# A 512-token transformer chain on one core: what stands at its stage boundaries

## The reference

```
# first block (8 heads per branch)
proj = rmsnorm(x) @ w_in       # A q,k,v | B q,f,i,g | C c_q,c_kv,k_rope | 3 gates
y_a = chunked_relpos_attention(a_q, a_k, a_v, rel_bias)
y_b = hgrn2_recurrence(b_q, b_f, b_i, b_g, ...)
y_c = mla_attention(c_q, c_kv, k_rope, ...)   # q = rmsnorm(c_q) @ w_uq, rotated
x = x + sum(sigmoid(gate_n) * (y_n @ w_branch[n])) @ w_out
x = x + relu(h2 @ w_ff1)**2 @ w_ff2
x = rmsnorm(x)
# second block, for each of two layers
x = x + mixer(rms_norm(x))     # stick-breaking, then differential attention
h = rms_norm(x)
x = x + (silu(h @ w_gate) * (h @ w_up)) @ w_down
```

## Time and profile before

| | |
|---|---|
| median of 3 runs | 2430.44 us (2429.25 to 2431.67) |
| the profiled execution's own time | 2428.63 us |
| its span | 2426.7 us |
| TensorE busy | 2289.7 us, 94% |
| VectorE, ScalarE, GpSimd busy | 1271.0, 932.8, 253.4 us |
| mean granted TensorE clock | 0.984 |

### The profile page before, as it was taken

One profiled execution on the slowest core, in us unless ns is written; L12 is line 12 of the kernel. 1 busy time (PEld: TensorE's weight loads), 2 busy tenths in 40 slices (PEclk: granted clock), 3 DMA queues, 4 the chain that ended last, 5 costly groups with the idle time before them and its releaser, 6 DMA issues.

```text
span 2426.7 us, 26942 instructions
## 1 busy us (share of the span) xinstructions
PE 2289.7 (94%) x10372; PEld 1779.0 (73%) x10372; DVE 1271.0 (52%) x2010; ACT 932.8 (38%) x1558; POOL 253.4 (10%) x422
## 2 busy tenths in 40 slices
PE   7999999898999999999998899999999888999999
PEld 6767777665888888877564688888776656888887
DVE  4574564355554544463444555555545766555554
ACT  4353332444443323242535433333344544433332
POOL 0000121220210000020313200000133201000000
PEclk9999999999999999999999999999999999999999
DMA  4212101211322222322110132323222101233223
GB/s 160 70 44 74 48 27 40 75 42 44 122 96 96 96 99 91 105 78 87 36 61 18 53 101 96 99 96 96 87 70 70 52 27 44 96 96 104 96 96 104
DMA packets 52110, 187.47 MB, mean 77 GB/s; under 512 B 5904, under 2 KB 6032, under 8 KB 51856
## 3 DMA queue, kind: packets, MB, share of 16 engines
q1 hardware_dynamic: 51984, 185.76, 23.5%
HBM read 183.64 MB, written 2.10 MB: 77 GB/s over the span
## 4 chain that ended last, share of the span: by engine, by line
PE 82%; ACT 6%; DVE 5%; POOL 3%; issue 3%; DMA 0%; POOLq 0%; DVEq 0%; SPq 0%; ACTq 0%
PE ps L774 20%; PE ps L777 20%; PE ps L775 20%; PE ps L795 3%; PE ps L798 3%; PE ps L796 3%; PE ps L865 2%; PE ps L897 2%; PE ps L759 2%; PE ps L943 1%; PE ps L974 1%; ACT W L1386 1%; ACT W L1384 1%; PE ps L1075 1%; ACT wh L1140 1%
## 5 line engine op out<-in xcount | busy, mean ns | idle before, releaser
L774 PE MATMUL ps<-hh,wl 128*128 128x512 f32 x1408 | 570.8, 405 | 21.9 <-DVE wl L1438 11.6
L1438 DVE TENSOR_TENSOR wl<-raw,wh 128x1024 fp32r<-128x1024 f32 (+1 forms) x336 | 421.4, 1254 | 301.8 <-ACT wh L1140 301.2
L777 PE MATMUL ps<-hl,wh 128*128 128x512 f32 x1408 | 552.7, 393 | 0.0
L775 PE MATMUL ps<-hh,wh 128*128 128x512 f32 x1408 | 552.2, 392 | 0.0
L1140 ACT CAST wh<-raw 128x1024 fp32r<-128x1024 f32 (+1 forms) x336 | 350.6, 1044 | 408.7 <-PE ps L777 315.5
L774 PE MATMUL ps<-R,wl 128*128 128x512 f32 x896 | 362.7, 405 | 4.3 <-issue 3.6
L777 PE MATMUL ps<-R,wh 128*128 128x512 f32 x896 | 352.4, 393 | 0.0
L775 PE MATMUL ps<-R,wh 128*128 128x512 f32 x896 | 351.8, 393 | 0.0
L774 PEld LDWEIGHTS ps<-hh,wl 128*128 128x128 f32 x1408 | 267.1, 190 | 83.6 <-issue 28.3
L777 PEld LDWEIGHTS ps<-hl,wh 128*128 128x128 f32 x1408 | 266.6, 189 | 58.0 <-DVE hl L1516 0.4
L775 PEld LDWEIGHTS ps<-hh,wh 128*128 128x128 f32 x1408 | 267.2, 190 | 54.9 <-issue 2.6
(11 more groups left out here) (225 smaller groups left out, 2376.7 us busy)
## 6 DMA issues: line engine op xcount, KB each, us to landing
raw<-in_weights SPq DMA_DIRECT2D x332, 512.0 KB, 3.3
x<-in_x_t SPq DMA_DIRECT2D x4, 512.0 KB, 6.4
F<-in_x_t SPq DMA_DIRECT2D x4, 512.0 KB, 5.3
out<-x SPq DMA_DIRECT2D x8, 256.0 KB, 2.0
raw<-in_weights SPq DMA_DIRECT2D x4, 416.0 KB, 3.2
x<-in_bias SPq DMA_DIRECT2D x1, 1024.0 KB, 6.0
C<-in_consts SPq DMA_DIRECT2D x1, 832.0 KB, 6.7
F<-in_weights SPq DMA_DIRECT2D x2, 384.0 KB, 3.6
```

Of the source, the lines that this page charges most:

```text
L774: pe.matmul(out, lo[:, k, cs], xh, start=k == 0, stop=False)
L775: pe.matmul(out, hi[:, k, cs], xh, start=False, stop=False)
L777: last = pe.matmul(out, hi[:, k, cs], xl, start=False, stop=k == u.nk - 1)
L1438: dve.tensor_tensor(lo, src, hi.bitcast(F32), ALU.subtract).then_inc(S[name], 1)
```

## The change

Seven edits to the plan, none of which adds or removes a dense matmul.

1. The last units of a stage take banks of their own where the next stage takes others: the last unit of A's projections and that of `uv[0]` take 0, 1, 6, 7; `bf` takes 4, 5, 6, 7; the q, k, v units `ud[0]` of differential attention go through six banks.
2. The recurrence's last four steps move from the end of uGA into uC, and the rest is spread at 44/48 instead of 48/48. uC takes banks 0, 1, 4, 5.
3. `c_norm` makes its eight squares first, then two logarithms and one exponential for all four token tiles. Before, it made two of each for every tile. Its squares go to W4 to W7, and VectorE's scaling waits for all of them.
4. In the latent branch each group's order is now `c_q`, `c_kv`, `c_qt`, `c_kt`, and `c_turn` begins one step later.
5. GpSimd rotates the queries two token tiles at a time: 12 operations per group on 128 columns, where 24 on 64 stood.
6. Group two's sixteen steps are attached to steps 4 to 19 of attention C0. Its heads go to F4 and F0 instead of F1 and F3, so that C0 can still read its own. The ratio is 66/48 instead of 75/48, since 19 ticks of side work have gone; attention C1 then ends with uGB.
7. The gated feed-forward's chunks have 2, 4, 4, 4, 4 and 4 tiles.

```diff
+C_HEADS = (("F1", "F3"), ("F4", "F0"))
...
     def mla(self):
+
+        def steps(g):
+            return [[(n, g, i)] for n in ("c_q", "c_kv", "c_qt", "c_kt") for i in range(4)]
+
+        yield []
         yield []
         for j in range(3):
             yield [("c_turn", j)]
         yield [("c_rope",)]
-        for g in range(2):
-            for tt in range(4):
-                yield [("c_q", g, tt)]
-            yield []
-            yield []
-            for h in range(4):
-                yield [("c_qt", g, h)]
-            for tt in range(4):
-                yield [("c_kv", g, tt)]
-            for h in range(4):
-                yield [("c_kt", g, h)]
-            yield from self.attn(ATTN[f"C{g}"])
+        yield from steps(0)
+        extra = [[]] * 4 + steps(1)
+        for i, tick in enumerate(self.attn(ATTN["C0"])):
+            yield tick + (extra[i] if i < len(extra) else [])
+        yield from self.attn(ATTN["C1"])
...
-                up, nj, f = [], 4 if c < 5 else 2, 8 + 6 * idx + c
+                up, k0, nj, f = [], max(4 * c - 2, 0), 4 if c else 2, 8 + 6 * idx + c
                 self.f_tile.append(tile)
                 for j in range(nj):
-                    gate = rows(("w_gate_2", idx), 0, 8, c * 512 + j * P, P, ("h", e), "fgate", wk=(4 * c + j) % 8)
-                    up += [gate, rows(("w_up_2", idx), 0, 8, c * 512 + j * P, P, ("h", e), "fup", gate=gate,
-                                      wk=(4 * c + j) % 8, f=f, j=j, tile=tile + j)]
-                ff.append((up, self.out(("w_down_2", idx), 4 * c, nj, ("f", f), norm=norm if c == 5 else None,
+                    c0, wk = (k0 + j) * P, (k0 + j) % 8
+                    gate = rows(("w_gate_2", idx), 0, 8, c0, P, ("h", e), "fgate", wk=wk)
+                    up += [gate, rows(("w_up_2", idx), 0, 8, c0, P, ("h", e), "fup", gate=gate, wk=wk, f=f, j=j,
+                                      tile=tile + j)]
+                ff.append((up, self.out(("w_down_2", idx), k0, nj, ("f", f), norm=norm if c == 5 else None,
                                         ship=idx == 1 and c == 5)))
                 tile += nj
...
-        self.run(self.dense(uA, roots(0, True) | {6: [("late",)], 9: [("late2",)]}))
+        self.run(self.dense(uA[:8], roots(0, True) | {6: [("late",)], 9: [("late2",)]}))
+        self.banks = (0, 1, 6, 7)
+        self.run(self.dense(uA[8:]))
         self.banks = (2, 3)
         self.run(interleave(self.dense(uB), self.attn(ATTN["A"]), 37 / 32))
         self.banks = (0, 1, 2, 3)
-        self.run(self.dense(uF))
+        self.run(self.dense(uF[:1]))
+        self.banks = (4, 5, 6, 7)
+        self.run(self.dense(uF[1:]))
         self.banks = (0, 1)
-        self.run(interleave(self.dense(uGA), self.hgrn(), 48 / 48))
-        self.banks = (0, 1, 2, 3)
-        self.run(self.dense(uC))
+        recurrence = list(self.hgrn())
+        self.run(interleave(self.dense(uGA), iter(recurrence[:-4]), 44 / 48))
+        self.banks = (0, 1, 4, 5)
+        self.run(self.dense(uC, {2 + 2 * i: t for i, t in enumerate(recurrence[-4:])}))
         self.add("c_norm")
         self.banks = (2, 3)
-        self.run(interleave(self.dense(uGB), self.mla(), 75 / 48))
+        self.run(interleave(self.dense(uGB), self.mla(), 66 / 48))
         self.banks = (0, 1, 2, 3)
         self.run(self.dense(uGC, {10 + 8 * i: [("again", i)] for i in range(4)}))
         self.run(self.dense(uO))
         self.run(self.dense(chain(ff1), roots(1)))
-        self.run(self.dense(uq[0] + uk[0] + uv[0], roots(2, True)))
+        self.run(self.dense(uq[0] + uk[0], roots(2, True)))
+        self.banks = (0, 1, 6, 7)
+        self.run(self.dense(uv[0]))
         self.banks = (2, 3)
         self.run(interleave(self.dense(uq[1] + uk[1]), self.sb(0), 18 / 32))
         self.banks = (0, 1, 2, 3)
...
         self.run(self.dense(uoS[1]))
         self.run(self.dense(chain(ff2a), roots(3)))
         self.add("zero", "F1", "F2")
+        self.banks = (0, 1, 2, 3, 4, 5)
         self.run(self.dense(ud[0], roots(4, True)))
+        self.banks = (0, 1, 2, 3)
         self.add("zero", "F5", "F6")
...
     def c_norm():
+        at.wait_ge("hg_s", 28)
         for tt in range(4):
-            o, w, s = B.F["F4"][:, tt * 416:(tt + 1) * 416], B.V(tt), B.stat(tt)
+            o, w, s = B.c_tokens()[:, tt, :], B.W[4 + tt], B.stat(tt)
             at.wait_ge(*plan.freed(plan.uC[0], tt)[0])
-            at.wait_ge("yb_l", 4)
             act.activation(w[:, 0:256], o[:, 0:256], ACT.Square, accum_out=s[:, 0:1]).then_inc(S["c_n"], 1)
             act.activation(w[:, 256:384], o[:, 256:384], ACT.Square, accum_out=s[:, 1:2]).then_inc(S["c_n"], 1)
-            for i, n in ((0, 256), (1, 128)):
-                at.wait_ge("c_n", 6 * tt + 1 + i)
-                act.activation(s[:, 2 + i:3 + i], s[:, i:i + 1], ACT.Ln, bias=eps, scale=1.0 / n).then_inc(S["c_n"], 1)
-                at.wait_ge("c_n", 6 * tt + 3 + 2 * i)
-                act.activation(s[:, 2 + i:3 + i], s[:, 2 + i:3 + i], ACT.Exp, scale=-0.5).then_inc(S["c_n"], 1)
+        s = B.st[:, 0:32].rearrange("p (t c) -> p t c", t=4)
+        at.wait_ge("c_n", 8)
+        act.activation(s[:, :, 2:3], s[:, :, 0:1], ACT.Ln, bias=eps, scale=1.0 / 256).then_inc(S["c_n"], 1)
+        act.activation(s[:, :, 3:4], s[:, :, 1:2], ACT.Ln, bias=eps, scale=1.0 / 128).then_inc(S["c_n"], 1)
+        at.wait_ge("c_n", 10)
+        act.activation(s[:, :, 2:4], s[:, :, 2:4], ACT.Exp, scale=-0.5).then_inc(S["c_n"], 1)
...
             if g:
-                at.wait_ge("at_o", ATTN["C0"].head(3))
+                at.wait_ge("c_t", 3)
+                at.wait_ge("c_rp", 6)
...
-            at.wait_ge("c_n", 6 * tt + 4)
+            at.wait_ge("c_n", 11)
             dve.tensor_scalar(o[:, 0:256], o[:, 0:256], s[:, 2:3], None, ALU.mult).then_inc(S["c_u"], 1)
-            at.wait_ge("c_n", 6 * tt + 6)
             dve.tensor_scalar(o[:, 256:384], o[:, 256:384], s[:, 3:4], None, ALU.mult).then_inc(S["c_u"], 1)
...
     def c_q(g, tt):
-        n = 24 * g + 6 * tt
-        o = B.c_heads("F0", tt)
-        w = B.F["F8"][:, 1280 + 256 * (tt % 2):1536 + 256 * (tt % 2)]
-        tmp = [w[:, 64 * i:64 * i + 64].rearrange("p (h r) -> p h r", h=4) for i in range(4)]
-        cos, sin = (B.misc_part(m).rearrange("p (t r) -> p t r", t=4)[:, tt, :].unsqueeze(1).to_broadcast([P, 4, 16])
+        if tt % 2 == 0:
+            return
+        o = B.F["F0"][:, (tt - 1) * 384:(tt + 1) * 384].rearrange("p (t h d) -> p t h d", t=2, h=4)
+        tmp = [B.F["F8"][:, 1280 + 128 * i:1408 + 128 * i].rearrange("p (t h r) -> p t h r", t=2, h=4) for i in range(4)]
+        cos, sin = (B.misc_part(m).rearrange("p (t r) -> p t r", t=4)[:, tt - 1:tt + 1, :].unsqueeze(2).to_broadcast([P, 2, 4, 16])
                     for m in ("cosA", "sinA"))
         at.wait_ge("c_qa", 4 * g + tt + 1)
-        rotate(o[:, :, 64:80], o[:, :, 80:96], o[:, :, 64:80], o[:, :, 80:96], cos, sin, tmp, "c_qp", n)
+        rotate(o[:, :, :, 64:80], o[:, :, :, 80:96], o[:, :, :, 64:80], o[:, :, :, 80:96], cos, sin, tmp, "c_qp",
+               12 * g + 6 * (tt // 2))
 
     def c_kv(g, tt):
```

15 lines of the change are left out of this document (9 added, 6 removed).

## The result

| | before | after |
|---|---|---|
| median of the runs | 2430.44 us (2429.25 to 2431.67) | 2438.39 us (2436.00 to 2444.00) |
| ratio to before, 95% interval | | 1.0036 (1.0025 to 1.0048) |
| profiled execution: span, clock | 2426.7 us, 0.984 | 2436.7 us, 0.981 |
| TensorE busy | 2289.7 us | 2298.9 us |

A forecast was written before the change was run, and what follows sets the result against it. TensorE was taken as the bound (busy 2289.7 of 2426.7 us), leaving its idle and half-clock time to win. Terms -7.6 - 0.8 - 2.5 - 1.1 + 1.5 - 4.5 + 2.0 = -13.0 gave a 2417.4 us median, range 2404 to 2427.

The forecast's parts named there:

- The short chunk first, six banks behind it: End of first gated feed-forward: late bank release behind the norm shrinks, -7.6 us (-9.2 to -5); kernel's end costs nothing.
- Banks of their own: Four other seams (behind A's projections, behind `uv[0]`, twice in `ud[0]`): 0.2 us each, -0.8, between 0 and -3.7.
- `bf`: Gate units: wait moves from bank to weights, half of the later `h_turn` wait goes; -2.5 us, between 0 and -3.5.
- The recurrence's end: In uC: its first matmul's wait goes, -1.1 us; moved `h_state` steps delay `h_out`, +1.5, between 0 and +5.
- `c_norm` and group one: Latent group one: shorter `c_turn` wait, rotation waits gone, new bank wait of 2.5; -4.5 us, between 0 and -7.
- Group two inside C0: Attention C0: sixteen steps wait 14.0 us for shared banks, 1.5 left in C1, against 13.5 lost before: +2.0 us.
- a low clock through C0: Many short waits make the clock fall across both attentions, 11.5 us lost: 2428.9, no change; chance 0.11.
- The slower rival: In C0, hand-overs cost like the dearest; at 2.4 us each the kernel takes 2441.8 us; chance 0.06.
- The signs of being wrong: Wrong if group two's waits add to half or double 14 us, or the norm's seam keeps 3 us.

## Why the prediction was wrong

Three steps of the sum failed: nothing was put for the last feed-forward's new order (it cost 5.0 us), the hand-overs in C0 were too small, and the clock was left out of the values. Of the loss 7 us more stand in stages that no edit explains. Taken by its own steps:

- *The short chunk first, six banks behind it* (-7.6): right for the first gated feed-forward, -8.2 in each profile. For the last one the step said "at the kernel's end the additions alone follow each tile, and they kept up before", and put the cost at nothing. **That conclusion failed.** The additions did keep up; what did not was the weight load, behind output transfers on SP's queue: +5.0, shown by the run that moves only those transfers. I had walked through VectorE's and ScalarE's queues at this place and not SP's.
- *Banks of their own* (-0.8) and *`bf`* (-2.5): the wait moved from the bank to the weights as forecast, 7.38. But the later wait shrank only to 0.71 and at another place, so 8.0 us of waits became 8.1. With the recurrence whole the same banks do give 1.7 (6.3 us of waits instead of 8.0), less than the 2.5 of the term; with the next edit beside them nothing is left.
- *The recurrence's end* (-1.1, +1.5): waits of 3.88, 2.83, 2.83 and 2.64 add up to 1.1 more than before, where 1.5 was forecast, and uC's 0.92 went as the -1.1 said. **The half-level clock behind them was put into the bound (+5) and not into the value**; measured, the part costs some 4.5 in all.
- *`c_norm` and group one* (-4.5): right in its waits, 2.15 at `c_turn` and 2.02 at `c_kv`, with those for the rotations gone. At 74 and 82 ticks over 48 the wait at `c_turn` is 3.0 to 3.6 in seven profiles, so the 2.15 holds for this spacing only.
- *Group two inside C0* (+2.0): **the walk through the hand-overs mis-sized the projections.** The transposes were put at 6.0 and waited 5.2. The scores behind `c_kv` were put at 2.3 and waited 2.9. The four `c_q` were put at 3.4, 0.2, 1.3 and 0.2 and waited 3.43, 1.45, 1.04 and 2.20: I charged ScalarE's queue, which was right for the first, and left out that at the second and the fourth the exponential itself waits for the row maximum. 16.2 instead of 14.0 in listed waits, and the clock, for which the term had nothing: 6.8 us lost in the stretch, 2.1 more than before. The sign was right. What the forecast did not see is how good the alternative was: the other latent edits without this move are worth 12 us.
- *The rivals*: "a low clock through C0" had a clock of 0.87 over the 40 us of the projections, but not by its mechanism, many short waits: the half level came at the two waits of 3.43 and 2.12. And it was too small to matter alone (6.8 lost against 4.6 before). The slower rival had the right sign and, at a measured 1.0 us a hand-over instead of 2.4, the wrong size.
- *The signs of being wrong*: neither of the two that were named came up. Group two's waits lay between half and double of 14 us and the norm's seam kept no wait of 3 us; neither sign covered the kernel's end or the clock.

The upper end, 2427, had room for one dear part and not for three. Of the 23 us between the forecast span change and the measured one, 5.0 lie at the end, some 6 in the latent stretch, 5.5 ahead of `c_turn`, 5.5 in differential attention and 1.6 in stick-breaking. That is 23.6, less the 0.5 by which the norm seam gave more. The last two, 7.1 us, are not explained by an edit: differential attention ran at 269 to 277 with the same waits, and stick-breaking, in which only the banks of `uv[0]` changed, lost 3.4 to the clock (before none) while its waits shrank by 1.2; with the same banks it took 334.3 in other profiles.

## What to carry to other kernels

When a last stage is reordered, walk the DMA-issuing queue as well: a transfer that waits for a result holds back every weight load behind it (5 us here, from a queue that looked idle). Work that is moved into an attention loop and shares its score banks pays for the whole chain from scores over the row maximum to the exponential (a dense piece between hid it at one of three places); keeping the same projections out and ordering them so that nothing waits for a rotation, with merged roots and rotations, gave 12 us instead. And take a bundle of edits apart: here the parts were worth about -8 (the norm seam), -12 (the latent edits with group two in sequence), -2 to -5 (the early banks), +5 (the last feed-forward's order), +5 (the recurrence's end) and +18 (group two inside C0, against that sequence), and the version that keeps the first three runs in 2407 us.
